# One transformer kernel: the second block's input projection on split operands, with weights that three engines prepare

## The reference

```python
h = rmsnorm(x, ln1_g)
proj = h @ w_in                        # 256 x 1024 by 1024 x 5632
q_sb, k_sb, v_sb, q_hg, f_hg, i_hg, g_hg, gate_sb, gate_hg = jnp.split(proj, splits, axis=-1)
y_sb = stick_breaking_attention(sb_heads(q_sb), sb_heads(k_sb), sb_heads(v_sb))       # 8 heads of 64
f = lb + (1.0 - lb) * jax.nn.sigmoid(f_hg.astype(f32))                                # forget gates
o = hgrn2_chunk_scan(hg_heads(silu(q_hg)), hg_heads(1.0 - f), hg_heads(log(f)), hg_heads(i_hg))
...
merged = sigmoid(gate_sb) * (y_sb @ w_branch_sb) + sigmoid(gate_hg) * (y_hg @ w_branch_hg)
return x + merged @ w_out
```

## Time and profile before

| | us |
|---|---|
| times of three runs | 2042.7, 2044.86, 2047.17 |
| median | 2044.86 |
| span of the profiled execution | 2042.8 |
| PE busy, all of the span | 1845.0 |
| DVE busy | 1086.0 |
| ACT busy | 759.2 |
| POOL busy | 86.2 |
| stretch from the first product of the projection to the first of `across` | 1450.88 to 1660.24 |

### The profile page before, as it was taken

One profiled execution on the slowest core, in us unless ns is written; L12 is line 12 of the kernel. 1 busy time (PEld: TensorE's weight loads), 2 busy tenths in 40 slices (PEclk: granted clock), 3 DMA queues, 4 the chain that ended last, 5 costly groups with the idle time before them and its releaser, 6 DMA issues. The chain is left out here.

```text
span 2042.8 us, 24685 instructions
## 1 busy us (share of the span) xinstructions
PE 1845.0 (90%) x8906; PEld 1411.4 (69%) x8906; DVE 1086.0 (53%) x2319; ACT 759.2 (37%) x1026; POOL 86.2 (4%) x49
## 2 busy tenths in 40 slices
PE   4999887999998666999999999999897989699997
PEld 2877443787887555778888888888675877544443
DVE  2469554211599998767667676766223532311112
ACT  1110248101101786346666666565255130111111
POOL 1200000000000443000000000000000000000000
PEclk8999888999999787999999999999898999699999
DMA  7466120042443000555555555554432323389993
GB/s 285 178 247 247 62 82 1 36 170 103 165 164 144 0 0 0 185 185 178 191 186 185 185 186 187 191 191 152 185 124 83 124 83 126 165 359 417 407 405 158
DMA packets 33318, 343.34 MB, mean 168 GB/s; under 512 B 3952, under 2 KB 4464, under 8 KB 5104
## 3 DMA queue, kind: packets, MB, share of 16 engines
q1 hardware_dynamic: 31680, 338.70, 43.5%
q10 hardware_dynamic: 1584, 3.90, 0.5%
HBM read 340.49 MB, written 2.10 MB: 168 GB/s over the span
## 5 line engine op out<-in xcount | busy, mean ns | idle before, releaser
L499 PE MATMUL psD<-xh,ring 128*128 128x256 f32 x1984 | 444.5, 386 | 19.0 <-DVE arena L1854 5.4
L499 PEld LDWEIGHTS psD<-xh,ring 128*128 128x128 f32 x1984 | 380.8, 193 | 80.3 <-issue 20.7
L999 ACT ACTIVATE arena<-psD 128x512 f32<-128x512 f32 (+6 forms) x243 | 147.0, 630 | 700.4 <-PE psD L499 501.5
L743 PE MATMUL psY<-ring_r,work_r 128*128 128x512 f32 x1536 | 372.2, 395 | 4.2 <-DVE ring_r L1675 3.5
L743 PEld LDWEIGHTS psY<-ring_r,work_r 128*128 128x128 f32 x1536 | 280.8, 189 | 71.3 <-issue 8.1
L999 ACT ACTIVATE ring_r<-ring 128x1024 fp32r<-128x1024 f32 x220 | 223.0, 1054 | 122.9 <-PE psY L743 62.3
L729 PE MATMUL psD<-xh_r,ring_r 128*128 128x512 f32 x736 | 262.6, 397 | 0.0
L731 PE MATMUL psD<-xh_r,ring_r 128*128 128x256 f32 x736 | 206.4, 280 | 0.0
L499 PE MATMUL psD<-arena,ring 128*128 128x256 f32 (+1 forms) x768 | 182.3, 399 | 15.6 <-DVE arena L1493 5.7
L499 PEld LDWEIGHTS psD<-arena,ring 128*128 128x128 f32 (+1 forms) x768 | 146.3, 192 | 50.9 <-issue 16.4
L1675 DVE TENSOR_TENSOR ring_r<-ring,ring_r 128x1024 fp32r<-128x1024 f32 x128 | 156.3, 1221 | 10.4 <-ACT ring_r L999 10.4
(11 more groups left out here) (222 smaller groups left out, 1584.4 us busy)
## 6 DMA issues: line engine op xcount, KB each, us to landing
ring<-in_tables SPq DMA_DIRECT2D x92, 1024.0 KB, 4.8
ring<-in_experts SPq DMA_DIRECT2D x24, 2048.0 KB, 9.4
arena<-in_experts SPq DMA_DIRECT2D x24, 2048.0 KB, 14.3
ring<-in_w_in SPq DMA_DIRECT2D x20, 2048.0 KB, 8.1
ring<-in_w_mod SPq DMA_DIRECT2D x12, 2048.0 KB, 8.1
ring<-in_early_u SPq DMA_DIRECT2D x9, 2048.0 KB, 8.0
ring<-in_early_v SPq DMA_DIRECT2D x18, 1024.0 KB, 4.8
ring<-in_w_out SPq DMA_DIRECT2D x4, 2048.0 KB, 7.9
```

Of the source, the lines that this page charges most:

```text
L499: last = nc.tensor.matmul(dst, a, b, start=(i == 0), stop=(i == len(pairs) - 1))
L743: last = nc.tensor.matmul(psY[:, t * D + h * 512:t * D + (h + 1) * 512], wgt[:, b, t * P:(t + 1) * P], v[:, h * 512:(h + 1) * 512], start= ...
L999: return nc.scalar.activation(dst, src, f, **kw)
```

## The change

The projection is computed from split operands. ACT rounds the normed tokens to `h2_hi` (eight copies) and DVE subtracts to get the low part. The weights are split in quarters of a block, 128 x 1024, 44 in all: POOL copies a quarter, rounded, to one of three buffers `in2_hi`, and DVE's `in2_rest` subtracts it from the ring's slot, in place. For each product of before PE computes three rounded ones with 256 columns (high by high, high by low, low by high), 48 per half block (`in2_half`), or half as many with 512 columns where tokens are the output rows. The loop over the contraction is now outside, with all 512 output columns of a block open in two banks of `psY`, which the projection has for itself; `psD` is left to the attention and the levels. ACT copies two banks per block (`in2_out`). The order of z, p and l stays, but six halves instead of six pairs come first, and DVE splits the two quarters for the next half at each p and in each level. The forget gates' chain is cut in two pieces, which stand behind the z of heads 6 and 7.

```diff
@@ -113,9 +114,11 @@
     order = [("z", 0), ("z", 1)]
     for h in range(SBH):
-        order += [("p", h), ("l", h)]
+        order += [("p", 6 + h), ("l", h)]
         if h + 2 < SBH:
             order.append(("z", h + 2))
+        if h in (4, 5):
+            order.append(("decay", h - 4))
     return order
...
@@ -148,13 +151,11 @@
     add("scores", 8, "act")
     add("trans", 2, "dve")
-    add("qks", 4, "act")
-    add("vs", 2, "act")
     for kind, n in second_order():
-        add(f"{kind}{n}", 1, "act" if kind == "p" else "dve")
+        if kind in "zl":
+            add(f"{kind}{n}", 1, "dve")
     for level in range(LEVELS + 1):
         add(f"level{level}", 4, "dve")
-        add(f"p{8 + level}", 1, "act")
     add("across", 2, "dve")
...
+        *in2_hi, h2_hi, in2_hi2 = rounded(("in2_hi0", 2304, D), ("in2_hi1", 3328, D), ("h2_hi", 18688, K, T),
+                                          ("in2_hi2", 30976, D))
+        in2_hi.append(in2_hi2)
...
-            for m in range(4):
-                wt = use(STREAM["w_in2"] + m // 2)
-                pair(TILE["qks"] + m, wt, 2 * (m % 2), hT, 1 if m == 2 else 0, None if m else (h_part, K))
-            def by_token(n, wt, t, frees):
...
+            def in2_half(half):
+                b = half // 2
+                tiles = [aux(2 * (b % 2) + j) for j in range(2)]
+                if half % 2 == 0 and b >= 2:
+                    pe.wait_ge(in2_copied, 2 * b - 2)
+                w_lo = ring_r[(IN2 + b) % RING]
+                for q in range(2 * half, 2 * half + 2):
+                    pe.wait_ge(in2_lo_ready, q + 1)
+                    w_hi = in2_hi[q % 3]
+                    for k in range(2 * (q % 4), 2 * (q % 4) + 2):
+                        if b == 0:
+                            pe.wait_ge(h2_split, k + 1)
+                        for i in range(2 if b in BY_TOKEN else 4):
+                            for hi, x in ((True, h2_hi), (True, h_lo), (False, h2_hi)):
+                                first = hi and x is h2_hi
+                                if b in BY_TOKEN:
+                                    wt = w_hi[:, (k % 2) * 512:(k % 2 + 1) * 512] if hi else w_lo[:, k * 512:(k + 1) * 512]
+                                    last = nc.tensor.matmul(tiles[i], x[:, k, i * P:(i + 1) * P], wt,
+                                                            start=(k == 0 and first), stop=(k == K - 1),
+                                                            skip_group_check=True)
+                                else:
+                                    wt = (w_hi[:, (k % 2) * 512 + i * P:(k % 2) * 512 + (i + 1) * P] if hi
+                                          else w_lo[:, k * 512 + i * P:k * 512 + (i + 1) * P])
+                                    last = nc.tensor.matmul(tiles[i // 2][:, (i % 2) * T:(i % 2 + 1) * T], wt, x[:, k, :],
+                                                            start=(k == 0 and first and i % 2 == 0), stop=(k == K - 1),
+                                                            skip_group_check=True)
+                                if b and k == 0 and i == 0 and first:
+                                    last.then_inc(w_used, 1)
+                    last.then_inc(in2_done, 1)
+            for half in range(6):
+                in2_half(half)
             pe.wait_ge(in_cst2, 48)
-            pe.wait_ge(blk2["qks"], 4)
+            pe.wait_ge(in2_copied, 4)
             for kind, n in second_order():
-                i = TILE[f"{kind}{n}"]
+                i = TILE.get(f"{kind}{n}")
                 if kind == "p":
-                    wt = use(STREAM["w_in2"] + 3 + n // 2)
-                    if n // 2 == 2:
-                        by_token(i, wt, n % 2, 1 - n % 2)
-                    else:
-                        pair(i, wt, 2 * (n % 2), hT, 1 - n % 2)
...
-                pair(TILE[f"p{n}"], use(STREAM["w_in2"] + 3 + n // 2), 2 * (n % 2), hT, 1 - n % 2)
+                in2_half(14 + level)
             pe.wait_ge(xl_ready, 8)
             for half in range(2):
                 ps = tile(TILE["across"] + half)
...
+                act.wait_ge(h_part, K + k + 1)
+                fn(h2_hi[:, k, :], hT[:, k, :], ACT.Copy).then_inc(h2_hi_ready, 1)
...
+            def in2_out(b):
+                act.wait_ge(in2_done, 4 * b + 4)
+                for i in range(2 * b, 2 * b + 2):
+                    fn(places[i], aux(i % 4), ACT.Copy, scale=SBD ** -0.5 if i < 2 else 1.0).then_inc(in2_copied, 1)
+            for b in range(3):
+                in2_out(b)
             for kind, n in second_order():
                 if kind == "p":
-                    ps = take(i)
-                    if n // 2 == 2:
...
                     fn(z[:, 1, :], z[:, 1, :], ACT.Ln, bias=1.0).then_inc(sp_ready, 1)
-                else:
+                elif kind == "l":
                     act.wait_ge(arg_ready, n + 1)
                     fn(sba[:, n, :], sbz[:, n % 2, 4, :], ACT.Exp).then_inc(a_exp, 1)
-            act.wait_ge(tile_free["act"], readers[:TILE["level0"]].count("act"))
-            fn(flat(fh), flat(fh), ACT.Sigmoid).then_inc(blk2["sig"], 1)
-            fn(flat(qh), flat(qh), ACT.Silu).then_inc(blk2["qh"], 1)
-            act.sem_inc(blk2["ih"], 2)
-            act.wait_ge(f_ready, 1)
-            fn(flat(lf), flat(fh), ACT.Ln).then_inc(lf_ready, 1)
+                elif n == 0:
+                    act.wait_ge(in2_copied, 10)
+                    fn(flat(fh), flat(fh), ACT.Sigmoid).then_inc(blk2["sig"], 1)
+                    fn(flat(qh), flat(qh), ACT.Silu).then_inc(blk2["qh"], 1)
+                else:
+                    act.wait_ge(f_ready, 1)
+                    fn(flat(lf), flat(fh), ACT.Ln).then_inc(lf_ready, 1)
...
             for level in range(LEVELS + 1):
                 if level + 2 <= LEVELS + 1:
                     decays(level + 2)
-                ps = take(TILE[f"p{8 + level}"])
-                fn(flat(gates2[:, 2 * level:2 * level + 2, :]), ps[:, :], ACT.Copy).then_inc(tile_free["act"], 1)
+                if level % 2:
+                    in2_out(7 + level // 2)
...
@@ -1380,6 +1419,15 @@
             nc.gpsimd.tensor_copy(h_hi, hT).then_inc(h_hi_ready, 1)
             pool.wait_ge(h_hi_ready, 1)
             nc.gpsimd.tensor_tensor(h_lo, hT, h_hi.bitcast(F32), ALU.subtract).then_inc(h_split, 1)
+            pool.wait_ge(stat_ready, STATS.index("xb") + 1)
+            for q in range(44):
+                slot = (IN2 + q // 4) % RING
+                if q % 4 == 0:
+                    pool.wait_ge(w_loaded[slot], 16 * ((IN2 + q // 4) // RING + 1))
+                if q >= 3:
+                    pool.wait_ge(in2_done, q - 2)
+                nc.gpsimd.tensor_copy(in2_hi[q % 3], ring[slot][:, (q % 4) * D:(q % 4 + 1) * D]).then_inc(in2_hi_ready, 1)
...
@@ -1747,6 +1795,19 @@
             dve.wait_ge(x_ready, 3 * K)
             inverse("xb", D)
             normed(8, hT, lambda k: vcol("ln1_g", k), h_part)
+            for k in range(K):
+                dve.wait_ge(h2_hi_ready, k + 1)
+                tt(h_lo[:, k, :], hT[:, k, :], h2_hi[:, k, :].bitcast(F32), ALU.subtract).then_inc(h2_split, 1)
+            def in2_rest(q):
+                slot, at = (IN2 + q // 4) % RING, slice((q % 4) * D, (q % 4 + 1) * D)
+                dve.wait_ge(in2_hi_ready, q + 1)
+                tt(ring_r[slot][:, at], ring[slot][:, at], in2_hi[q % 3].bitcast(F32),
+                   ALU.subtract).then_inc(in2_lo_ready, 1)
+            for q in range(12):
+                in2_rest(q)
...
+            in2_rest(13)
             for kind, n in second_order():
                 i = TILE.get(f"{kind}{n}")
                 z = sbz[:, n % 2]
-                if kind == "z":
+                if kind == "p":
+                    in2_rest(2 * n + 2)
+                    in2_rest(2 * n + 3)
+                elif kind == "decay" and n == 0:
+                    dve.wait_ge(blk2["sig"], 1)
+                    for k in range(4):
+                        last = mark(ts(fh[:, k, :], fh[:, k, :], lbv[:, 5, k:k + 1], lbv[:, 3, k:k + 1],
+                                       ALU.mult, ALU.add))
+                    dve.wait_ge(dve_step, last)
+                    ts(flat(kh), flat(fh), -1.0, 1.0, ALU.mult, ALU.add).then_inc(f_ready, 1)
+                elif kind == "decay":
+                    dve.wait_ge(lf_ready, 1)
+                    seq(nc.vector.tensor_tensor_scan(flat(cum), reset, flat(lf), 0.0, ALU.mult, ALU.add))
+                elif kind == "z":
                     ps = take(i)
                     dve.wait_ge(sp_ready, n + 1)
                     mark(stt(z[:, 2, :], ps[:, 0:3 * P], 0.0, z[:, 1, :], ALU.min, ALU.subtract))
...
             tt(diagonal(sba[:, SBH - 1, :]), diagonal(sba[:, SBH - 1, :]), tri2, ALU.mult).then_inc(a_masked, 1)
-            dve.wait_ge(blk2["sig"], 1)
-            for k in range(4):
```

(6 more changed lines are left out.)

59 lines of the change are left out of this document (30 added, 29 removed).

## The result

The changed kernel took 2053.82 us, the median of four runs (2048.28, 2053.81, 2053.83 and 2054.32); the kernel before took 2043.9 in the four runs beside them. The ratio on record is 1.0041 (95% interval 1.0029 to 1.0053); the two medians alone would give 1.0049. I had forecast 2035.0, so the sign is wrong: 9.9 us slower instead of 9.9 us faster. Of the 3.7 us that its span is longer than that of the earlier trace rows, 8.1 are lost in the changed stretch, and 2.5 ahead of it and 2.0 behind it are won, where the code is the same.

What follows compares the result with a forecast made beforehand. PE was taken to bound the kernel, gapless in heads and levels. Level 1's half 10.7 us early, less 1.5, plus 1.2, less 0.5, gave 9.9 off 2044.86: 2035.0 us; own range 2028 to 2042, 8-in-10 range 2026 to 2047.

Steps and rivals of the forecast that it cites:

- Steps 1 and 2: Start and first six halves: PE's first product 7.2 us later, yet z of head 0 at 1494.6, 0.7 early.
- The hold between POOL and DVE: Each POOL cast holds DVE's splits, masks, exponents and gates, not moves out of PSUM; without it about 4 us less.
- Steps 3 and 4: Heads, then moved chain: 8.2 us a head to head 4, then 10.9, 10.2 and 5.6; last subtraction 1.9 later.
- step 4: Moved chain, heads 4 to 7 and after: half of level 1 starts at 1583.3 instead of 1594.03, 10.7 us early.
- slow starts: Behind PE's gaps of 3 to 4 us at heads 1, 6, 7 and level 1: 1 or 2 us, mostly hidden.
- Step 5: Levels: 10.1 us each against 9.85, six rounds lose 1.5; last half saves 1.2, ACT copies cost 0.5.
- ring: In each level: quarter, cast, split, exponents, moves, last tile and handovers wait in a circle, 10.1 us.
- The handshake does not bind: Rival for the whole stretch: PE stays without gaps, end 38 us early, 2007; chance 0.06.
- Slow cast: Rival on POOL: the cast takes 1.9 us as its TENSOR_TENSOR does, 13.3 lost, 2048.3; chance 0.12.
- 0.13: Rival on PE: 256 columns take 0.13 us, near the upper bound; 5.6 us less gain, 2040.6; chance 0.12.
- a load does not fit: Rival on PE: a load does not fit beneath 256 columns and takes 0.19; about 38 slower, 2083; chance 0.04.
- The move brings nothing: Rival on the chain: ACT's Sigmoid and Silu delay the heads by what they save behind; 2040 to 2044; chance 0.06.

Runs made afterwards that it cites:

- experiment 1: Changed kernel, but in each level DVE does the exponents and four moves first and the two splits for the next half last: 2022.79 us, ratio 0.9896.
- Experiment 2: Changed kernel with twelve more unneeded products on PE ahead of each level's tiles from level 1 on, DVE's order kept: 2035.78 us, ratio 0.9953.
- experiment 4: Changed kernel with a fourth place for the cast blocks from the levels on, DVE's order kept: 2029.72 us.
- experiment 6: Changed kernel with the forget gates' chain back behind the heads, split projection kept: 2051.3 us.
- experiment 8: Kernel of experiment 1 with a gap put back: ACT copies 128x1400 behind each half of the levels and PE's next tiles wait: 2028.1 us.
- experiment 9: Kernel of experiment 8 with another 1200 columns copied for level 1 alone, lengthening the first gap: 2040.12 us, median of ten.
- experiment 10: Kernel of experiment 8 with 1700 columns copied instead of 1400, so longer gaps in each level: 2036.92 us.
- experiment 11: Changed kernel with twelve more products on PE ahead of level 1 alone, later gaps kept: 2053.03 us.
- experiment 12: Kernel of experiment 8 with three more ACT copies, one for each of tiles 1 to 3 to wait for: 2057.8 us, ratio 1.0059.
- experiment 5: Kernel before the change with only the forget gates' chain moved, projection on unsplit operands: 2033.63 us, ratio 0.9946.
- experiment 7: Kernel of experiment 1 with the forget gates' chain back behind the heads: 2026.13 us.

## Why the prediction was wrong

*Steps 1 and 2* held: first product 0.7 early, z 1.8 early. Quarters are 0.120 apart per product, 2.88 each (forecast 0.118), the cast is 1.04 (forecast 1.0), the split 1.22:

```profile
L1430 POOL CAST in_hi<-ring x44: 1037/1042/1922, 1445.1 to 1649.2; 128x1024 fp32r<-128x1024 f32 x44
```

The hold between POOL and DVE is there as well. A mask of 128x256 that takes 0.42 took 1.08 and ended just behind the cast that it fell into. A split that began inside a cast took up to 2.09 instead of 1.22, and one that began ahead of the cast kept its 1.22. Casts that began among DVE's instructions took up to 1.92 here and 5.28 in experiment 1. In these rows whoever starts first holds the other.

```profile
1542.03 1.04 POOL L1430 CAST in_hi<-ring 128x1024 fp32r<-128x1024 f32 x1 [1.68 <-PE psY L825]
...
1542.26 1.08 DVE L1850 TENSOR_TENSOR arena<-arena 128x256 f32<-128x256 f32 x1
```

Two splits of the weights, where a cast ran beside the second, take 3.22 us instead of 2.35:

```profile
1508.81 3.22 DVE L1806 TENSOR_TENSOR ring_r<-ring,in_hi 128x1024 fp32r<-128x1024 f32 x2
...
1509.92 1.04 POOL L1430 CAST in_hi<-ring 128x1024 fp32r<-128x1024 f32 x1 [1.84 <-PE psY L831]
```

*Steps 3 and 4* held in this trace: 8.45 from head to head instead of 8.2, with DVE idle for ACT; 10.6, 10.6 and 5.9 around the chain instead of 10.9, 10.2 and 5.6; the half of level 1 1.2 us earlier than forecast. A part of that is in my addition: step 4's own terms give 1581.6 to 1582.9 and not 1583.3. The slow starts that I put "mostly beneath DVE's chain" are not always hidden: stretches at a clock of 0.50, more of them or longer ones, go with the 3.7 us by which the heads of other traces are longer.

*Step 5* failed. Its ring is real, link by link: 10.25 us in the level that kept its clock, against 10.1. But I summed it at full clock. The prediction named a slow start behind "gaps of 3 to 4 us at heads 1, 6, 7 and level 1" and took none behind the 1.5 us of each level, which it had counted itself. The five rounds from the half of level 1 to that of level 6 took 66.4 us instead of 50.5, which is 15.9 or some 3.2 a round, and the last two levels lost another 3.3, 19.2 us in sum. The term taken at nothing stands on the ring, where products that run at half speed delay the cast, the split and the moves. Experiment 2 shows that the clock carries it: with the gap filled, and the ring and its order kept, a level takes 10.5. Experiments 1 and 4 show that the ring makes the gap. Why the clock falls behind one gap of some 1.5 us and not behind another is not shown (experiments 6 and 8 to 12).

*The rivals.* "The handshake does not bind" was given 0.06; it did bind, and opening it by an order of DVE took one edit. "Slow cast", "0.13" and "a load does not fit" are refuted by the records: 1.04, and 0.120 between products. "The move brings nothing" is half right: 10.0 us without the split (experiment 5), 3.3 with it and no gaps (experiment 7). Up to the half of level 1, at 143.8 before, the traces have 134.1 with the move alone (experiment 5), 138.6 with the split alone (experiment 6) and 131.9 with both: gains of 9.7, 5.2 and 11.9, which overlap and do not add. What the split gave up to there it lost in the levels. None of the rivals had the granted clock as its mechanism, and that was the one that decided.

## What to carry to other kernels

When a change puts a wait on TensorE into a loop, price the loop twice, at full clock and with the products behind the gap at half clock, above all where the waiting engine feeds what TensorE waits for: then the slow products lengthen the ring itself. Look for what stands ahead of the releasing instruction on its engine: here two splits ahead of four moves cost 31 us, and putting them behind cost nothing. A gap that can't be removed can be filled with products whose result nobody reads, which saved 18 us here. That it helps to end it in one piece, with all that follows ready, rests on one comparison (experiments 8 and 12) in which the missing time was not held equal.
